# Moving means of a pooling branch: band-matrix products on TensorE, or shifted additions on GpSimd over turned input

## What is computed

```python
c_q, c_kv, k_rope, dq, dk, dv, p_in, z_gate = jnp.split(z, split_idx, axis=-1)

def pool_mixer(p, pool_w, pool_b, pool_scale):     # POOL_WINDOWS = (2, 4, 8, 16)
    cs = jnp.cumsum(pf, axis=1)
    for g, w in enumerate(POOL_WINDOWS):
        c = cs[..., g * 128:(g + 1) * 128]
        prev = jnp.pad(c, ((0, 0), (w, 0), (0, 0)))[:, :s]
        cnt = jnp.minimum(t + 1, w)
        outs.append((c - prev) / cnt - pf[..., g * 128:(g + 1) * 128])
    y = jnp.einsum('bsgc,gcd->bsgd', pooled, pool_w) + pool_b
    return y.reshape(b, s, 512) * pool_scale

branches = jnp.einsum('bsnc,ncd->bsnd', [y_mla, y_diff, y_pool], w_branch[l])
merged = jnp.sum(sigmoid(z_gate) * branches, axis=2)
h = h + merged @ w_out[l]
```

## Time and profile before

| | |
|---|---|
| median of 3 runs | 2056.66 us (2056.29 to 2057.01) |
| profiled execution | 2056.99 us |
| its span, first to last instruction | 2055.2 us |
| PE busy | 2040.3 us, 99% |
| DVE busy | 1390.4 us, 68% |
| ACT busy | 1018.4 us, 50% |
| POOL busy | 76.0 us, 4% |
| granted clock of TensorE, mean | 0.998 of full speed |

### The profile page before, as it was taken

How to read it: one execution, slowest core, us unless ns; L and a number is a source line. 1 busy time by engine, 2 the same in 40 slices (tenths; PEclk the granted TensorE clock), 3 DMA queues, 4 the chain that set the end, 5 groups by cost and what they waited for, 6 DMA issues and landing times.

```text
span 2055.2 us, 25142 instructions
## 1 busy us (share of the span) xinstructions
PE 2040.3 (99%) x10357; PEld 1718.7 (84%) x10357; DVE 1390.4 (68%) x1638; ACT 1018.4 (50%) x1290; POOL 76.0 (4%) x119
## 2 busy tenths in 40 slices
PE   9999999999999999999999999999999999999998
PEld 7888888888888888888888888888888888888887
DVE  6545686775757666787575667657767667577676
ACT  6444486454435345675444365644534466544331
POOL 1000000000010001000100000000100000000000
PEclk9999999999999999999999999999999999999999
DMA  8655454475656555544666474554755645455552
GB/s 311 209 188 184 164 170 144 137 222 186 193 189 223 187 177 193 171 141 147 204 198 190 159 243 144 177 164 167 239 190 186 204 154 185 156 191 186 194 193 83
DMA packets 223729, 377.20 MB, mean 184 GB/s; under 512 B 6544, under 2 KB 109072, under 8 KB 223616
## 3 DMA queue, kind: packets, MB, share of 16 engines
q1 hardware_dynamic: 219504, 362.31, 53.6%
q0 software_dynamic: 3824, 12.97, 2.1%
q10 hardware_dynamic: 288, 0.33, 0.1%
HBM read 374.53 MB, written 1.05 MB: 183 GB/s over the span
## 4 chain that ended last, share of the span: by engine, by line
PE 95%; DVE 2%; ACT 1%; DMA 1%; issue 0%; POOL 0%; DVEq 0%; ACTq 0%
PE pb L1585 63%; PE pb L1596 16%; PE pb L1599 9%; PE pb L1608 2%; DMA raw<-in_ffn_w_up_dram 1%; PE pb L1654 1%; DVE wl L2054 0%; PE pb L1732 0%; DVE lS L2241 0%; ACT wh L1826 0%; DVE st L2247 0%; DVE st L2246 0%; DMA raw<-in_ffn_w_gate_dram 0%; PE pb L1719 0%; PE pb L1796 0%
## 5 line engine op out<-in xcount | busy, mean ns | idle before, releaser
L1826 ACT ACTIVATE wh<-raw 128x2048 fp32r<-128x2048 f32 (+4 forms) x351 | 658.6, 1877 | 640.2 <-PE pb L1585 284.5
L2054 DVE TENSOR_TENSOR wl<-raw,wh 128x2048 fp32r<-128x2048 f32 (+4 forms) x351 | 783.1, 2236 | 167.6 <-ACT wh L1826 166.9
L1585 PE MATMUL pb<-wh,x 128*128 128x512 f32 (+1 forms) x2224 | 676.3, 386 | 0.0
L1585 PEld LDWEIGHTS pb<-wh,x 128*128 128x128 f32 x2224 | 415.7, 188 | 80.9
L1585 PE MATMUL pb<-wl,x 128*128 128x512 f32 (+2 forms) x1112 | 438.8, 395 | 0.1
L1596 PE MATMUL pb<-x,wh 128*128 128x512 f32 x1504 | 379.6, 394 | 0.0
L1596 PEld LDWEIGHTS pb<-x,wh 128*128 128x128 f32 x1504 | 271.5, 189 | 49.5
L1585 PE MATMUL pb<-wl,mh 128*128 128x512 f32 (+1 forms) x740 | 255.8, 391 | 0.9 <-issue 0.9
L1585 PE MATMUL pb<-wh,ml 128*128 128x512 f32 (+1 forms) x740 | 253.7, 388 | 0.0
L1585 PE MATMUL pb<-wh,mh 128*128 128x512 f32 (+1 forms) x740 | 253.5, 388 | 0.0
L1585 PEld LDWEIGHTS pb<-wl,x 128*128 128x128 f32 x1112 | 208.9, 188 | 45.0 <-issue 3.7
(11 more groups left out here) (361 smaller groups left out, 1581.0 us busy)
## 6 DMA issues: line engine op xcount, KB each, us to landing
raw<-in_w_in_dram SPq DMA_DIRECT2D x100, 1024.0 KB, 5.2
raw<-in_w_ff_dram SPq DMA_DIRECT2D x64, 1024.0 KB, 5.2
raw<-in_ffn_w_down_dram SPq DMA_DIRECT2D x44, 1024.0 KB, 4.9
raw<-in_ffn_w_up_dram SPq DMA_DIRECT2D x43, 1024.0 KB, 5.4
raw<-in_ffn_w_gate_dram SPq DMA_DIRECT2D x42, 1024.0 KB, 5.3
raw<-in_w_branch_dram SPq DMA_DIRECT2D x24, 1024.0 KB, 5.0
raw<-in_w_out_dram SPq DMA_DIRECT2D x16, 1024.0 KB, 5.0
raw<-in_w_in_dram SPq DMA_DIRECT2D x4, 832.0 KB, 4.5
```

The lines of the kernel that those rows point to most:

```text
L1585: ins = e.matmul(pb[b][:, 0:c1 - c0], x[:, s, cols], w[:, n, c0:c1], start=(it["first"] and n == 0 and q == 0), stop=(it["stop"] and n == ...
L1826: e.activation(hi, raw, ACT.Copy).then_inc(m.high_done, 1)
L2054: e.tensor_tensor(lo, raw, hi.bitcast(F32), ALU.subtract).then_inc(m.low_done, 1)
```

## The change

The pool input is computed turned, by `copy_w(1952, "pT", pin)`, in the place where the `dv` group was; the `dv` group moves up to where the pool input's was. `pT` is now a view of a buffer `pp` with 16 columns of zeros ahead of each group's 256. The lane `pool` begins with an item `windows`: GpSimd sets the zeros and makes the running sums of 2, 4, 8 and 16 positions by four additions of an array to itself shifted by 1, 2, 4 and 8, and corrects the first 16 positions of each group by factors from a small table `short`, loaded once by GpSimd's queue (four multiplications 128x16). The item `pooling` on DVE (L2205 in the changed kernel, four SCALAR_TENSOR_TENSOR of 128x256) scales each sum and subtracts the input, waiting for `summed`. `poolsum`, `poolcopy`, the table c_pool and the loop that pumped until the pooling was done are gone, and so is the weighing's wait for `pin`. `poolmix`, `poolbias` and `poolsplit` are unchanged but for layout, and lie where the lane now emits them.

```diff
-        self.group(self.cols(W, l, 0, 0, c_epi, 416) + self.cols(W, l, 1952, 1, self.copy_t("pin", pin)), start=True)
+        self.group(self.cols(W, l, 0, 0, c_epi, 416) + self.cols(W, l, 1440, 1, self.copy_t("dv", self.dv)), start=True)
         while len(scaled) < 2:
             self.pump()
-        pool_done = []
 
         def pool():
+            self.add("windows", need=list(pin))
+            for _ in range(4):
+                yield
+            self.add("pooling", n=l)
             yield
             yield
             for i in range(2):
                 use = self.side()
-                v = self.pe("poolsum", i=i, use=use, need=list(pin), l=l)
-                self.add("poolcopy", i=i, use=use, p=v["p"])
-                got = use
-                yield
-            self.pin_free = [v["p"]]
-            for i in range(2):
-                use = self.side()
-                v = self.pe("poolmix", i=i, use=use, need=[("evac", got)], l=l)
+                v = self.pe("poolmix", i=i, use=use, need=[("pooled", l + 1)], l=l)
                 self.add("poolbias", i=i, use=use, p=v["p"], l=l)
                 yield
             self.add("poolsplit", use=use, n=l)
...
-            self.kt_free = v["p"]
-            pool_done.append(True)
-
-        self.lanes[3].append(pool())
...
-        self.group(self.cols(W, l, 1440, 0, self.copy_t("dv", self.dv)))
-        while not pool_done or ("C", 2, 1) not in self.ready or ("C", 2, 0) not in self.ready:
+        self.copy_w(1952, "pT", pin)
+        self.lanes[3].append(pool())
+        while ("C", 2, 1) not in self.ready or ("C", 2, 0) not in self.ready:
             self.pump()
         self.add("krrope", n=l, need=[self.ready["C", 2, 0], self.ready["C", 2, 1]])
...
-        while not self.pin_free or len(self.dv) < 2:
+        while len(self.dv) < 2:
...
-            e.dma_start(m.pc[:, :], m.A["c_pool"]).then_inc(m.pc_landed, 16)
...
+        elif k == "windows":
+            pp, sa, sb, end = m.pp, m.sa, m.sb, 16 + S
+            po.all_ready(it["need"])
+            po.step(e.memset(pp[:, :, 0:16], 0.0))
+            po.own_steps()
+            po.step(e.tensor_tensor(sa[:, :, 1:end], pp[:, :, 1:end], pp[:, :, 0:end - 1], ALU.add))
+            po.own_steps()
+            po.step(e.tensor_tensor(sb[:, :, 3:end], sa[:, 1:4, 3:end], sa[:, 1:4, 1:end - 2], ALU.add))
+            po.own_steps()
+            po.step(e.tensor_tensor(sa[:, 2:4, 7:end], sb[:, 1:3, 7:end], sb[:, 1:3, 3:end - 4], ALU.add))
+            po.own_steps()
+            po.step(e.tensor_tensor(sb[:, 2, 15:end], sa[:, 3, 15:end], sa[:, 3, 7:end - 8], ALU.add))
+            po.own_steps()
+            po.wait_ge(m.short_landed, 16)
+            sums = m.window_sums()
+            for g in range(4):
+                ins = e.tensor_tensor(sums[g][:, 0:16], sums[g][:, 0:16], m.short[:, g, :], ALU.mult)
+            ins.then_inc(m.summed, 1)
...
+        elif k == "pooling":
+            v.wait_ge(m.summed, n + 1)
+            for g, x in enumerate(m.window_sums()):
+                ins = e.scalar_tensor_tensor(m.pT[:, g, :], x, 0.5 ** (g + 1), m.pT[:, g, :], ALU.mult,
+                                             ALU.subtract)
+            ins.then_inc(m.pooled, 1)
```

More of the change, by code:

```diff
@@ L45, in constants @@
     freq = np.broadcast_to(np.stack([f1, f1, f2, f2]).reshape(1, 64), (P, 64))
-    pool = np.zeros((256, 4, 256), np.float64)
-    for g, w in enumerate((2, 4, 8, 16)):
-        for t in range(256):
-            lo = max(0, t - w + 1)
-            pool[lo:t + 1, g, t] += 1.0 / (t + 1 - lo)
-            pool[t, g, t] -= 1.0
-    pool = pool.astype(np.float32)
-    p0 = pool[0:128].reshape(P, 1024)
-    p1 = pool[128:256, :, 128:256].reshape(P, 512)
+    short = np.array([[w / min(t + 1, w) for t in range(16)] for w in (2, 4, 8, 16)], np.float32)
     s = q[:, None]
@@ L179, in sbuf @@
         self.bn = A("bn", take(128), [P, 2, 16])
+        self.short = A("short", take(256), [P, 4, 16])
         self.epsc = A("epsc", take(32), [P, 8])
@@ L2217, in dve_program @@
         elif k == "poolsplit":
-            pT, hi, lo = [w[:, :, :].rearrange("p a s -> p (a s)") for w in (m.pT, m.yph, m.ypl)]
             v.wait_ge(m.pool_high, n + 1)
-            e.tensor_tensor(lo, pT, hi.bitcast(F32), ALU.subtract).then_inc(m.pool_low, 1)
+            e.tensor_tensor(m.ypl[:, :, :], m.pT[:, :, :], m.yph[:, :, :].bitcast(F32), ALU.subtract).then_inc(m.pool_low, 1)
         elif k == "krrope":
```

43 lines of the change are left out of this document (15 added, 28 removed).

## The result

The changed kernel took 2085.68 us (median, 2084.6 to 2086.01) beside 2056.65 us of the kernel before (2056.29 to 2057.01): a ratio of 1.0139, 95% interval 1.0127 to 1.0151. The prediction was 2087.1. The profiled execution has a span of 2082.8 us against 2055.2, 27.6 more.

A forecast was written before the change was run, and what follows sets the result against it. PE, busy 99% of the span, was taken as the bound. Per layer 14.1 - 3.5 - 0.6 + 1.2 + 1.7 + 2.3 = 15.2, twice 30.4, gave 2087.1 us; range 2075 to 2097.

The forecast's parts named there:

- the wait for `ypl`: PE's branch product waits for DVE's low half of the pool output: start +14.1 us a layer, about 10 of it idle.
- What PE is spared: Pooling sums gone (2.44), weight products moved (1.36), wide form +0.3: PE 3.5 us early at first, per layer.
- GpSimd's hold of DVE: GpSimd's first addition holds up DVE's two-input operations at krrope: 2.3 us a layer, all on the chain to ypl.
- The reductions: Three of the pool input's four reductions on DVE ahead of krrope: 2.07 us a layer, all on the path.
- DVE's idle 1.01 us takes up the first bias: DVE's idle time at 294.77, ahead of the third combination, absorbs 1.01 us of the added DVE work.
- the fourth pair's wait: At the fourth pair's turn PE waits for DVE, delayed by a low half and a merge: +1.2 us a layer.
- The clock: PE's granted clock falls after the long idle wait at the branch: +1.7 us a layer, between 0 and 3.4.
- c_pool's load: GpSimd's queue loses a 786 KB load per layer; nothing waits for it, so 0.
- A: Rival: DVE is never held up by GpSimd, the 2.3 goes, 12.9 a layer, 2082.5 us; chance 0.25.
- B: Rival: GpSimd's sums come late, +10 a layer, 2107 us, or more is lost, 2092 to 2096; chance 0.13.
- C: Rival: DVE keeps up and only the sums' removal is left, 2.1 a layer gained, 2052.5 us; chance 0.04.
- D: Rival: ypl in time by 10 us, but reductions stay on the chain, 1.1 a layer, 2059 us; chance 0.03.

The follow-up runs named there:

- Experiments 1 and 2: 1: kernel before with twelve more lane steps between sums and poolmix, 2079.14 us; 2: changed kernel with the pooling's second half directly behind the first, 2060.75 us.
- experiment 3: Changed kernel with GpSimd's four additions cut to one column each and the buffers zero-filled, window sums left out of the result: 2084.89 us.
- Experiment 5: Changed kernel with the pooling's second half directly behind the first and krrope ahead of the pool input's wide group: 2059.95 us.
- experiment 7: Experiment 5's kernel with the pool input's products accumulated in the same 256 columns, copied by ACT without DVE reductions: 2053.37 us.
- experiment 4: Changed kernel reordered twice: pool input first, second dq/dk halves behind the first scores, 2067.44 us; all three wide groups and krrope ahead of the scores, 2065.69 us.

## Why the prediction was right, and where it was not

The time, 1.4 us off, and the main mechanism, the wait for `ypl` in either layer, were right. How near the time came is in part luck: some terms were wrong and made up for each other. By its own steps:

- **What PE is spared** was taken as 3.5 and is 4.3. The +0.3 for the wide form does not show. The other 0.5 is what the pieces taken out cost besides their own time: in the kernel before, the wide item behind a poolsum takes 2.89 (229.34 to 232.23) and the one behind a poolmix 2.98 (237.01 to 239.99), against 2.79 for one that follows another; twice 0.1 and twice 0.19 make 0.6, about that.
- **The wait for ypl** was right in place and size: a shift of 12.9 with the hold (14.1 - 3.5 + 2.3), measured 12.0; PE waits 8.74 and 8.75 us (10 foretold, 12 with the hold). From the third combination to the end of `ypl` I had 5.6 to 5.7 us, the trace has 302.14 to 307.68, 5.5. Experiments 1 and 2 show this place to be 22 to 25 of the 29 us.
- **GpSimd's hold of DVE**, "all of it on the chain that leads to ypl": the hold is there, 1.7 us (2.3 was taken), and the second addition and DVE's low half show the reverse. By the rule of the Trainium skill, "SBUF — State Buffer", section "Who interferes with whom", whoever of the two issues first blocks the other; both directions of it are now in rows (1.87 in place of 0.19, and 3.67 in place of the 1.53 of another run). But the step failed: experiment 3 takes the hold away and gains 0.8 us of the 3.4 that it should, since PE, slowed by the clock, is as late at kvk anyway.
- **The reductions**, "all on the path, as ACT already waits there": they cost what was said (1.28 + 0.68 = 1.96 on DVE, 2.07 taken), but by another way. They do not only delay krrope; they also free the PSUM banks late. I had read the order of DVE only for what waits for its data, not for who waits for its banks. From the first scores to the copies behind kvk the changed kernel takes 22.03 us (243.28 to 265.31), the kernel before 18.56 (249.27 to 267.83), so 3.5 are lost. Experiment 5, with neither hold nor fall of the clock in its first layer, takes 20.96 (243.63 to 264.59): 2.4 go with the wait for the banks, and the other 1.1 with the hold or the clock, which do not add up. That is a little less than reductions and hold together would have made (2.0 + 1.7); experiment 7 shows the wait to be for the reductions. One term too many and one missing thus cancelled: a right number for a partly wrong reason.
- **DVE's idle 1.01 us takes up the first bias**: it did not. The third pair's scores now wait 1.46 for the bank that this bias frees (L1643 at 293.63), and DVE idles 1.14, about as before. This too is a wait for a bank.
- **L2205 and the first bias** took 1.34 and 0.99 (1.65 and 1.0); **the turns** -0.6 and **the fourth pair's wait** 1.06 (1.2) as said.
- **The clock**, 1.7 a layer from the trace's start: 2.7 in the first layer, 1.4 in the second, for the same wait of 8.7 us. The loss at the trace's start, from which I took the size, is made up again by 22 us; behind the long wait nothing makes it up. The second fall, at the query product, cost nothing beside the hold.
- **c_pool's load**, "neither is waited for, 0": I had not looked at the waits ahead of the mixer. The changed kernel gains 1.7 there, 1.1 of it at the wait that goes with the load; without them the time would have come out at about the forecast's 2087.
- Of the rivals, A says rightly that the hold costs next to nothing here, though not for its reason (DVE is held), and at 2082.5 it is 3 us low, as the bank waits and the clock took more. B, C and D are out: the sums are ready 17 us early, and ypl is late by 9.

## What to carry to other kernels

What is saved on the bound engine can be lost many times over by moving a small step that had margin: 4.3 us a layer were saved on PE, and the branch still began 12 us later, because a small split on an engine 67% busy now stood behind a softmax in its queue, where before it had 52 us of margin. For each moved step ask twice what stands ahead of it in its engine's order: for the reader of its data, and for whoever wants the PSUM bank that it frees. The repair was one step of a lane (25 us), and then to give the evacuation to the engine that was free (6.6 us), not to move groups around it, which only moved the wait (experiment 4).
